# The first RMS norm of a decoder layer: how its squares are summed, and where the first weights are split

## The reference, cut to what matters

```python
def rmsnorm(x, g):
    y = xf * lax.rsqrt(jnp.mean(xf * xf, axis=-1, keepdims=True) + RMS_EPS)
    return (y * g.astype(jnp.float32)).astype(x.dtype)

def half_swiglu(x, g, w_gate, w_up, w_down):
    h = rmsnorm(x, g)
    return x + 0.5 * ((jax.nn.silu(h @ w_gate) * (h @ w_up)) @ w_down)
```

## Time and profile before

| | before |
|---|---|
| median of three runs | 1853.16 us |
| the profiled execution | 1854.38 us |
| span of its trace | 1852.6 us |
| TensorE busy | 1767.8 us (95%) |
| VectorE busy | 673.5 us (36%) |
| ScalarE busy | 610.6 us (33%) |
| GpSimd busy | 680.4 us (37%) |

### The profile page before, as it was taken

The page is one execution under the profiler, slowest core; times in us unless marked ns, Lnnn a source line. Parts: engine busy times, 40 slices in busy tenths (PEclk is TensorE's granted clock), DMA queues, the critical chain, the costliest instruction groups (busy, mean ns, idle before and its releaser), DMA issues.

```text
span 1852.6 us, 41879 instructions
## 1 busy us (share of the span) xinstructions
PE 1767.8 (95%) x17052; PEld 1683.7 (91%) x17052; DVE 673.5 (36%) x1110; ACT 610.6 (33%) x809; POOL 680.4 (37%) x816
## 2 busy tenths in 40 slices
PE   6999999998889999999999999999999999999999
PEld 5999999998888898988788989898899999999999
DVE  3222012212554545454465352626355222012210
ACT  4332122222432424242244343435234333123321
POOL 2455445443331313130122223224155545344543
PEclk9999999999989999999899999999999999999999
DMA  3334233332442215131154453545443334333343
GB/s 142 123 113 141 96 123 113 125 127 93 151 162 73 99 67 189 68 100 56 36 193 174 163 179 141 180 154 215 177 147 102 113 125 138 117 102 125 124 138 124
DMA packets 53112, 237.49 MB, mean 128 GB/s; under 512 B 7040, under 2 KB 7680, under 8 KB 51584
## 3 DMA queue, kind: packets, MB, share of 16 engines
q1 hardware_dynamic: 45120, 219.40, 34.3%
q10 hardware_dynamic: 7872, 16.37, 2.4%
HBM read 217.98 MB, written 71.76 MB: 156 GB/s over the span
## 4 chain that ended last, share of the span: by engine, by line
issue 45%; PE 26%; POOL 25%; ACT 1%; DVE 1%; POOLq 1%; DVEq 0%; ACTq 0%; DMA 0%
POOL w_lo L332 25%; PE ps L345 16%; PE ps L1672 1%; PE ps L791 1%; PE ps L1849 1%; PE ps L1717 1%; ACT w_hi L325 1%; PE ps L1787 1%; PE ps L1773 1%; PE ps L1757 0%; PE ps L1793 0%; ACT qkv L1459 0%; POOLq L647 0%; PE ps L1261 0%; PE ps L1750 0%
## 5 line engine op out<-in xcount | busy, mean ns | idle before, releaser
L332 POOL TENSOR_TENSOR w_lo<-w_raw,w_hi 128x256 fp32r<-128x256 f32 (+1 forms) x808 | 674.7, 866 | 1156.2 <-ACT w_hi L325 1156.2
L345 PE MATMUL ps<-h_hi,w_hi 128*128 128x288 f32 x2464 | 556.3, 308 | 32.2 <-POOL w_lo L332 17.8
L345 PE MATMUL ps<-h_hi,w_lo 128*128 128x288 f32 x2464 | 530.8, 297 | 0.0
L345 PE MATMUL ps<-h_lo,w_hi 128*128 128x288 f32 x2464 | 530.3, 297 | 0.0
L345 PEld LDWEIGHTS ps<-h_hi,w_hi 128*128 128x128 f32 x2464 | 400.3, 190 | 56.7 <-issue 20.4
L345 PEld LDWEIGHTS ps<-h_lo,w_hi 128*128 128x128 f32 x2464 | 400.1, 190 | 0.0
L345 PEld LDWEIGHTS ps<-h_hi,w_lo 128*128 128x128 f32 x2464 | 399.9, 190 | 0.0
L325 ACT ACTIVATE w_hi<-w_raw 128x1024 fp32r<-128x1024 f32 (+1 forms) x204 | 226.3, 1109 | 462.0 <-PE ps L345 445.4
L345 PE MATMUL ps<-g_hi,w_hi 128*128 128x288 f32 x704 | 151.6, 297 | 1.8 <-POOL w_lo L332 1.8
L345 PE MATMUL ps<-g_lo,w_hi 128*128 128x288 f32 x704 | 151.1, 296 | 0.0
L345 PE MATMUL ps<-g_hi,w_lo 128*128 128x288 f32 x704 | 151.0, 296 | 0.0
(11 more groups left out here) (364 smaller groups left out, 1867.5 us busy)
## 6 DMA issues: line engine op xcount, KB each, us to landing
w_raw<-in_w SPq DMA_DIRECT2D x172, 512.0 KB, 3.7
w_raw<-in_w SPq DMA_DIRECT2D x32, 704.0 KB, 4.0
kv<-in_kc SPq DMA_DIRECT2D x32, 576.0 KB, 6.1
kv<-in_vc SPq DMA_DIRECT2D x32, 576.0 KB, 6.9
cache_out<-in_cache SPq DMA_DIRECT2D x28, 576.0 KB
gates<-gate_out ACTq DMA_DIRECT2D x16, 288.0 KB, 2.6
cache_out<-in_cache SPq DMA_DIRECT2D x8, 480.0 KB
kvT<-qkv ACTq DMA_DIRECT2D x4, 864.0 KB, 4.8
```

The source lines that it names most:

```text
L332: last = nc.gpsimd.tensor_tensor(w_lo[par_][:, c], w_raw[par_][:, c], w_hi[par_][:, c].bitcast(F32), ALU.subtract)
L345: last = nc.tensor.matmul(ps[:, b + c, 0:HC], w[par_][:, wk], a[:, k, c * HC:(c + 1) * HC], start=(first and k == 0), stop=(end and k == n ...
```

## The change

The first norm is given the form of the other two, with nrt_first as the accumulator: square 0 is written into it, and VectorE adds squares 1 to 7 (add_square) behind each h_low. sum_squares and its eight products are gone; one sum_all (two matmuls) stands inside unit 1, ahead of its slice 3. ScalarE's wait for a square's buffer is now one for VectorE's add two tiles back. The split of the first weights stands right behind square 0, that of the second behind h_high of tile 4. The parameter table par is issued second, and counted with the first x tile; the constants come after all of x.

```diff
-        ACC = (None, nrt_first, mA)
+        ACC = (nrt_first, nrt_first, mA)
...
-            pe.wait_ge(sem("sq_added"), 7 * m)
+            pe.wait_ge(sem("sq_added"), 7 * m + 7)
...
-            if m:
-                if k == 0:
-                    out = ACC[m]
-                elif k >= 3:
-                    act.wait_ge(sem("sq_added"), 7 * (m - 1) + k - 2)
-            elif k >= 2:
-                act.wait_ge(sem("sq_summed"), k - 1)
+            if k == 0:
+                out = ACC[m]
+            elif k >= 3:
+                act.wait_ge(sem("sq_added"), 7 * m + k - 2)
...
             for k in range(KD):
                 if k % 2 == 0:
-                    act.wait_ge(sem("x_loaded%d" % (k // 2)), 16)
+                    act.wait_ge(sem("x_loaded%d" % (k // 2)), 16 if k else 32)
                 square(act, 0, k, k % 2)
+                if k == 0:
+                    split_hi(act, 0, 0, W8)
                 h_high(act, 0, k, k % 2)
-                if k in (1, 3):
-                    split_hi(act, 0, k // 2, W8)
+                if k == 4:
+                    split_hi(act, 0, 1, W8)
...
         def first_dve(dve, own):
-            dve.wait_ge(sem("con_loaded"), 32)
...
                 h_gained(dve, 0, k, "g1")
                 if k:
                     h_low(dve, 0, k - 1)
+                    if k > 1:
+                        add_square(dve, 0, k - 1)
             h_low(dve, 0, KD - 1)
+            add_square(dve, 0, KD - 1)
...
-            if f == 0:
-                pe.wait_ge(sem("con_loaded"), 32)
-                sum_squares(pe, 0, 0, 0, start=True)
             unit_wait(pe, P0, 0)
             for k in range(KD):
-                if f == 0 and k:
-                    sum_squares(pe, 0, k, k % 2, stop=(k == KD - 1))
...
-            unit(pe, P0, 1)
+            unit_wait(pe, P0, 1)
+            for k in range(KD):
+                if f == 0 and k == 3:
+                    pe.wait_ge(sem("con_loaded"), 16)
+                    sum_all(pe, 0)
+                last = unit_slice(1, h_hi, h_lo, k, k, KD, 2)
+            last.then_inc(unit_done, 1)
...
                 if i == 0:
-                    act.dma_start(con[:, 0:CFIRST], t["con"][:, 0:CFIRST]).then_inc(sem("con_loaded"), 16)
-                    act.dma_start(par[:, :, 0], t["par"]).then_inc(sem("con_loaded"), 16)
+                    act.dma_start(par[:, :, 0], t["par"]).then_inc(sem("x_loaded0"), 16)
+            act.dma_start(con[:, 0:CFIRST], t["con"][:, 0:CFIRST]).then_inc(sem("con_loaded"), 16)
```

More of the change, by code:

```diff
@@ L483, in first_act @@
                 if k % 2 == 0:
-                    act.wait_ge(sem("x_loaded%d" % (k // 2)), 16)
+                    act.wait_ge(sem("x_loaded%d" % (k // 2)), 16 if k else 32)
                 square(act, 0, k, k % 2)
+                if k == 0:
+                    split_hi(act, 0, 0, W8)
                 h_high(act, 0, k, k % 2)
-                if k in (1, 3):
-                    split_hi(act, 0, k // 2, W8)
+                if k == 4:
+                    split_hi(act, 0, 1, W8)
             root_act(act, own, 0)
         def first_dve(dve, own):
-            dve.wait_ge(sem("con_loaded"), 32)
             for k in range(KD):
                 if k % 2 == 0:
-                    dve.wait_ge(sem("x_loaded%d" % (k // 2)), 16)
+                    dve.wait_ge(sem("x_loaded%d" % (k // 2)), 16 if k else 32)
                 h_gained(dve, 0, k, "g1")
```

## The result

The changed kernel takes 1859.14 us, the median of 20 runs (1852.61 to 1866.70); the kernel before, run beside it, 1853.75 us (20 runs). The ratio is 1.0032, 95% interval 1.0018 to 1.0046: slower by 0.32% (+5.4 us), where the forecast was +3.1 us or 0.17%. The profiled execution took 1866.70 us with a span of 1864.9 us, so it lies 7.6 us above the median of its kernel, while that of before lay close to its own.

The account below looks back on a forecast made before the run. TensorE, busy 1767.8 of 1852.6 us, bounds the kernel, so only the start of unit 2 counts. Its +2.9 us and +0.2 of low clock, some 3.1 us on 1853.16, gave 1856.3 us, range 1852.6 to 1860.2.

Parts of the forecast that it names:

- the likeliest case: Whole kernel: the time stays the same, within 0.2% (3.7 us) of the kernel before; chance 0.59.
- What sets the end: Start of unit 2: it follows the sum of squares through one chain, 10.41 us today, less about 0.3.
- Table first: Start of the kernel: par, issued earlier, lands at 7.9 us against 8.7, and square 0 waits for it.
- Weights behind square 0: First weight split: GpSimd starts at 9.85 instead of 12.77, and unit 0 begins near 14.0, 2.2 us sooner.
- Seven additions on VectorE: Unit 0: VectorE's turn becomes 2.3 us and sets the pace; last h_lo at 28.7, last addition at 29.6.
- TensorE and its clock: Units 0 and 1: last slice at 1.2 GHz, clock back during unit 1, sum ready at 34.4 us.
- rival B: Units 0 and 1: clock holds at 2.4 GHz, sum ready at 33.0, +1.7 us, 1854.9; chance 0.15 together with another rival.
- The chain behind the sum: Root to unit 2: unit 2 starts at 44.55, +2.9 us; low clock behind the longer pause adds 0.2.
- The sum: Total: +2.9 and +0.2, some 3.1 us, giving a median of 1856.3 us.
- the forecast's own case: Unit 1: the clock comes back early there; spread about +1.5 to +4.7 us; chance 0.54.
- The prediction's own sign of being wrong: Unit 2 to the end: a length differing from today's 1811 us by more than a microsecond or two.
- Rival A: Units 0 and 1: clock stays at 1.2 GHz until the sum, ready at 36.7; +6.6 us, 1859.8; chance 0.23.

Follow-up runs that it names:

- Experiment 2: The change with the two weight splits back behind tiles 1 and 3, additions and single product kept: 1857.39 us, ratio 1.0022 to the kernel before.
- Experiment 4: The change with VectorE's seven additions left out, their semaphore steps kept: 1858.43 us, ratio 1.0023 to the kernel before.
- Experiment 12: The change with eight extra matmuls ahead of each of slices 3 to 7 of unit 0: 1851.60 us, ratio 0.9992 to the kernel before.
- experiment 9: The changed kernel measured a second time, without further edit, beside its form with 56 drains on one chip: 1857.62 us, ratio 1.0023 to the kernel before.
- experiment 3: The change with the single product ahead of unit 1's slice 0 instead of slice 3: 1856.94 us, ratio 1.0027 to the kernel before.
- the padded change: The change with 56 drains at the start of TensorE's list, measured twice: 1855.04 us (ratio 1.0013) and 1855.17 us (1.0012).
- experiment 6: The change with the cache copy issued ahead of the last weight pair instead of behind it: 1854.43 us, ratio 1.0001 to the kernel before.
- experiment 7: The kernel before with 200 drains in TensorE's list, 100 at its start and 100 behind the first barrier: 1856.02 us, ratio 1.0015.

## Why the prediction was right, and where it was not

The measured median lies in the range (1852.6 to 1860.2), but in the 0.38 that was given to slower by over 0.2%, not in the likeliest case. Step by step:

- **What sets the end.** Right: the start of unit 2 follows the sum by 10.32 us (34.78 to 45.10; 10.1 was forecast). In all fourteen profiles it lies 9.9 to 11.3 us behind the start of the root.
- **Table first.** 7.9 forecast, 8.16 measured.
- **Weights behind square 0.** Unit 0 at 14.0 forecast, 13.63 measured; the split beside VectorE took 3.51 us, not 4.1. But the text treated this as a gain with nothing to pay. Experiment 2 shows the price: with the split left where it was, the sum is ready 1.7 us sooner. The prediction did say that the first h_hi is pushed behind the weight copy, but counted this delay as part of the change and not as a cost of the split. Where VectorE sets the pace, each later tile inherits it: 1.25 of the 1.7 us. The rest is the pauses: it foresaw that they would bring the clock down, and did not ask whether fewer were to be had by starting later.
- **Seven additions on VectorE.** Right in kind and size: last h_lo forecast at 28.7, measured at 28.82, last addition 29.6 and 29.67. That the figure fits so well is in part luck: the first h_lo ended at 12.09, 0.4 us later than forecast, and the losses to GpSimd behind it were 2.0 us (four instructions with two inputs and two gains), 0.4 less than forecast. Experiment 4 puts the whole cost of the additions at 6.7 us of the start.
- **TensorE and its clock.** Right: the last slice at the low clock, the return inside unit 1, the sum at 34.4 forecast and 34.75 measured. Experiment 12 measures the term: 1.3 us of the sum, near the 1.4 us that lay between the forecast and rival B. The rule of the Trainium skill, "TensorE: Matmul & The Clock Gate", section "A second HAM failure mode: psum-queue depth-cycling", which the prediction names, agrees with this trace: the granted clock is 1.00 from 18.5 us and 0.50 from 21.9 to 32.1, once the slices wait.
- **The chain behind the sum.** +2.9 forecast for unit 2, +3.44 measured. The low clock behind the pause ran to about 49.2 us, 4.1 us of work instead of 3.5: +0.3, and 0.2 was forecast.
- **The sum.** The range held, but +5.4 us lies outside the +1.5 to +4.7 that the forecast's own case allowed, because a term was missing. The prediction held everything behind unit 2 to be unchanged but shifted. The change took 14 fp32 matmuls (28 matmul and 28 weight-load records) out of TensorE's program. The fetch of a later block then met the burst of a weight load and a cache copy near 850 us, which cost 6.5 to 10.2 us in the executions of experiments 4, 9 and 3 and of the change. The prediction's own sign of being wrong, another length of the stretch from unit 2 to the end, showed it in the first profile (1819.8 us) and missed it in the second (1810.3). By the differences of medians the padded change costs 1.8 and 2.1 us (1855.04 against 1853.28, 1855.17 against 1853.12), somewhat less than the forecast 3.1; unpadded it costs 5.4 and 4.5 us (1859.14 against 1853.75, 1857.62 against 1853.12).

Rival A, which had a price near what was measured (+6.6), did not happen in the first profile: the clock was back before the sum was made. In that of experiment 9 the matmuls ran at the low clock's pace (0.48 us a pair) from the first slice of unit 0 to 32.1 us, and the root still started at 34.77; A had the sum at 36.7. That its figure fits is chance.

What stays open. How often the stop occurs in the changed kernel is known only by its two profiles, which both have it, and by its slower runs; so it isn't known what share of the 2 us between the median's +5.4 and the start's 3.4 it makes. That a packet was late is seen in the traces; that the weight load and the copy delayed it follows from the table, from experiment 6 and from the place where it happens, but how the queues share the DMA engines was not measured. And experiment 7, which should have brought the stop to the kernel before, did not show it in its one profile.

## What to carry to other kernels

Before work is moved from a loaded engine to one that the whole profile calls idle (VectorE 36%), add up that engine's turn in the very loop it joins: here it went from 1.4 to 2.3 us and became the pace of a stage in which everything ends in one chain. Work that is moved forward must not push back the first input of the engine that sets the pace: here a weight copy ahead of the first h_hi cost that engine's whole chain over a microsecond. An engine that starts earlier than it can be fed buys pauses, and here the pauses brought its clock down for 10 us. And when a kernel with long straight code comes out slower than its changed stage explains, set equal places of both traces side by side and look for idle time by "issue": the number of instructions alone can move a fetch into a burst of transfers. Look at the place, in several executions: the totals of single profiles differ by more than the effect.

## What the runs showed of the hardware that was not expected

- TensorE stopped for 2.5 to 4.7 us in the middle of independent matmuls (2.54, 4.46, 4.73, 2.48 in four profiles), each time some five microseconds behind a weight load of 512 KB and a cache copy, issued 0.4 us apart, and each time at the same matmul of the program. None of the seven profiles whose packets fall as in the kernel before shows it.
- The stop's length follows the packet: 7.22 and 7.52 us behind the issue of the weight load gave 4.46 and 4.73 us, 5.39 and 5.45 gave 2.54 and 2.48, 3.14 gave 0.62, and 2.70 gave none.
- These four stops cost two to three times their length (6.5 to 10.2 us), since the clock fell behind them: in the change 18 us of mostly small matmuls ran at a granted clock of 0.50.
- 56 drains at the head of TensorE's list brought its packets back to the places of the kernel before, and the changed kernel from 5.4 to 1.8 us above it, and on one chip from 4.5 to 2.1 (medians; the intervals of the two forms overlap).
- 40 useless matmuls in the pauses of unit 0 kept the clock at its high level there and brought the sum forward by 1.6 us, 1.3 of it by the clock; by 60 us only 0.6 was left, since the clock stayed low for longer behind the next pause.
